# First expert stage of a two-block model: the first block's hidden products and the next gather placed ahead of the further blocks

## The chip, the cores and the metric

The kernel runs on one core of one Trainium2 chip. The metric is the time of one execution on the device in microseconds (us); lower is better. It computes in float32 throughout the part that is changed.

## The reference

Two model blocks in a row work on 256 tokens of width 1024: each is a token mixer (attention, in the first also a state-space branch) and then a mixture of experts. The change touches the first mixture alone. Each token chooses experts of one group among 32, and each expert is a gated unit of width 256:

```
def expert_block(args):
    xb, e = args
    return (jax.nn.silu(xb @ w_gate[e]) * (xb @ w_up[e])) @ w_down[e]

ys = lax.map(expert_block, (xs, blk_e)).reshape(P, D)
out = jnp.zeros((N, D), jnp.float32).at[buf_t].add(ys.astype(jnp.float32) * buf_w[:, None])
```

Here `xs` are the chosen tokens of each expert, and `buf_w` the weight with which a result is added back to its token.

## The kernel before, in words

**Groups and blocks.** The first expert stage handles the 32 experts in 8 groups of 4. The four experts of a group share TensorE's columns, 32 tokens each, so that one *block* serves 4 x 32 tokens. If an expert has more than 32 tokens, its group has *further blocks*. How many is counted on the chip (`block_tables`, L2119) and read from the small table `tabI` by each engine with two loads (L452, L453). `run_experts` (L446) is the loop that TensorE, ScalarE and VectorE all run: four passes with two groups each (u = 0 and 1); in each group first `begin`, then an `If` (L455) around the further blocks, and then the first block (`first`).

**Steps of a block on TensorE.** `gather_group` (32 products of the tokens `hN` with a matrix of ones and zeros) brings the block's tokens together; `hidden_group` (L1082, 128 products: 64 with the gate weights, then 64 with the up weights) fills one PSUM bank; `act_turn` and `spread_turn` transpose the activations and the matrix that spreads results; `down_group` (L1093, 32 products) and `scatter_group` (16 products) add the result to the tokens' sums. The first block is pipelined over groups: its tokens are gathered one group earlier (`gather_group` in `first`, L1189), and its results are scattered in the next group's `first` (L1194). A further block runs all its steps at once, ahead of the first block of its group, and waits between them for VectorE and ScalarE.

**Steps on the other engines.** VectorE makes the matrices of ones and zeros (`gather_onehot`, L2159; `spread_onehot`, L2170 and L2171), copies the hidden products out (`units`, L2204), half of the gathered tokens (`pair_out`, L2188) and the results (`ys_out`, L2194). ScalarE takes the sigmoid (L1681), the other half of the gathered tokens (L1669) and the transposed matrices. Each engine takes its instructions in order.

**Weights.** A ring of 12 slots of 1 MB holds exactly one group: 4 gate, 4 up and 4 down tiles. SyncE asks for the next group's tiles in that order (`load_moe1`, L484). It waits for a slot to come free in `free1` (L494): gate tiles for `gates_used`, which the first block's 64th hidden product counts up (L1090), up tiles for `hidden`, down tiles for `down`, all of the first block, which runs last in its group:

```
def free1(j, groups):
    sp.wait_ge((gates_used, s1["hidden"], s1["down"])[j // 4], groups)
```

After the eight groups SyncE asks for the tiles of the next dense stage with the same `free1`, for the slots that the last group leaves. The second expert stage (32 experts, `GROUP[2]` = 1) uses `run_experts` too.

## Time and profile before

| | us |
|---|---|
| median of 3 runs | 2052.98 |
| lowest and highest of them | 2050.46, 2053.23 |
| the profiled execution's own time | 2053.45 |
| its span (first to last instruction) | 2051.7 |
| TensorE busy in the span | 1832.5 (89%) |
| VectorE, ScalarE busy | 527.4, 390.7 |
| moved by the DMA engines | 626.77 MB, mean 305 GB/s |
| first expert stage, first gather to last scatter | about 433 to 726 |

Times in the views are microseconds from the span's start. PE is TensorE's array, PEld its weight loads (PEldq its sequencer), DVE VectorE, ACT ScalarE, SPq SyncE's queue. All matrix products carry L464, a helper's line, and all transposes L592, so that the steps are told apart by their tiles and counts: hidden products are x128 with 256 columns out of `ring`, down products x32 with 512, gathers x32 out of `hN`, scatters x16. The "idle before" of an instruction ends with what released it; "issue" means that the profile shows nothing it waited for. PEclk is the granted clock of TensorE as a share of 2.4 GHz.

### The profile page before, as it was taken

To read this page: it belongs to the slowest core of one execution; us is meant where nothing else is said; L and a number is where in the kernel's file an instruction comes from. 1 tells how busy PE (TensorE), PEld (TensorE's weight loads), DVE (VectorE), ACT (ScalarE), POOL (GpSimd) and SP (SyncE) were. 2 spreads that over 40 slices of the span, in tenths; PEclk is the share of its full clock that TensorE was granted. 3 is DMA by queue.
4 is the path that set the end of the run, shared out by engine and by line. 5 is a ranking of instruction groups with operands and counts; after the bars stand their busy time and mean duration, and the time that the engine had idled before them with its cause. 6 is when DMAs were issued, how large, how long until landed. Compare 5 with 4: busy or idle time off the path is not lost.

```text
span 2051.7 us, 27907 instructions
## 1 busy us (share of the span) xinstructions
PE 1832.5 (89%) x10699; PEld 1006.3 (49%) x10700; DVE 527.4 (26%) x1211; ACT 390.7 (19%) x905; POOL 50.2 (2%) x109
## 2 busy tenths in 40 slices
PE   6999899978667889999978999889988999989887
PEld 4665677855344566777844333333333333323332
DVE  3676332131111133232431111111111111111112
ACT  3132454021011130244020111111100111101111
POOL 0040000000000010010010000000000000000000
PEclk9999899998888999999989999999999999999999
DMA  9968622418999662232435999999999899999997
GB/s 399 403 230 346 271 82 84 162 63 334 394 411 409 267 215 87 65 100 98 152 149 208 416 417 417 417 417 418 416 416 419 323 418 417 416 417 417 416 416 297
DMA packets 108632, 626.77 MB, mean 305 GB/s; under 512 B 11200, under 2 KB 15296, under 8 KB 50080
## 3 DMA queue, kind: packets, MB, share of 16 engines
q1 hardware_dynamic: 106688, 620.10, 75.1%
q0 software_dynamic: 1584, 4.33, 1.3%
q8 instruction: 70, 1.15, 0.2%
q10 hardware_dynamic: 272, 1.05, 0.1%
q14 instruction: 18, 0.15, 0.0%
HBM read 624.39 MB, written 1.05 MB: 305 GB/s over the span
## 4 chain that ended last, share of the span: by engine, by line
PE 62%; DMA 20%; SPq 10%; issue 4%; DVE 2%; ACT 1%; DVEq 0%; ACTq 0%
PE ps L464 59%; DMA ring<-in_w_gu_dram 15%; SPq L517 5%; SPq L520 4%; PE ps L592 2%; DMA ring<-in_moe_w_gate_dram 1%; DMA ring<-in_w_dn_dram 1%; DMA ring<-in_ada_w_dram 1%; DMA ring<-in_w_mod_dram 1%; DMA ring<-in_moe_w_down_dram 1%; ACT arena L1403 1%; PE ps L839 0%; SPq L490 0%; SPq L421 0%; ACT hT L1730 0%
## 5 line engine op out<-in xcount | busy, mean ns | idle before, releaser
L464 PE MATMUL ps<-ring,arena 128*64 128x512 f32 (+2 forms) x5376 | 898.8, 558 | 123.7 <-issue 59.1
L464 PEld LDWEIGHTS ps<-ring,arena 128*64 128x64 f32 (+1 forms) x5376 | 291.7, 131 | 671.4 <-issue 482.2
L464 PE MATMUL ps<-arena 64*128 64x512 f32 (+11 forms) x1494 | 262.2, 417 | 36.7 <-ACT arena L1403 15.5
L464 PE MATMUL ps<-hT,ring 128*128 128x256 f32 (+1 forms) x960 | 237.2, 402 | 2.3 <-DVE hT L1864 2.3
L464 PEld LDWEIGHTS ps<-hT,ring 128*128 128x128 f32 x960 | 180.5, 192 | 58.8 <-issue 33.6
L464 PEld LDWEIGHTS ps<-arena 64*128 64x128 f32 (+7 forms) x1494 | 128.2, 159 | 154.5 <-issue 97.0
L2212 DVE TENSOR_SCALAR arena<-ps 128x512 f32<-128x512 f32 (+1 forms) x34 | 23.0, 676 | 535.3 <-PE ps L464 535.3
L1403 ACT ACTIVATE arena<-ps 128x256 f32<-128x256 f32 (+5 forms) x191 | 104.3, 570 | 267.7 <-PE ps L592 134.0
L1669 ACT ACTIVATE arena<-ps,mod,gain 128x128 f32<-128x128 f32 x176 | 66.1, 458 | 425.3 <-PE ps L464 425.3
L1681 ACT ACTIVATE arena<-arena 128x512 f32<-128x512 f32 (+1 forms) x44 | 25.3, 575 | 601.7 <-DVE arena L2212 400.7
L464 PEld LDWEIGHTS ps<-arena,hN 128*128 128x128 f32 x960 | 116.3, 200 | 42.2 <-issue 16.3
L464 PE MATMUL ps<-arena,hN 128*128 128x128 f32 (+1 forms) x960 | 124.8, 287 | 10.3 <-DVE arena L2159 5.7
L464 PE MATMUL ps<-ring,hT 128*128 128x256 f32 (+2 forms) x416 | 83.5, 380 | 5.8 <-ACT hT L1743 5.8
L592 PE MATMUL ps<-consts,arena 128*128 128x128 f32 x522 | 73.7, 278 | 9.2 <-DVE arena L2218 6.2
L464 PEld LDWEIGHTS ps<-ring,hT 128*128 128x128 f32 (+1 forms) x416 | 70.6, 187 | 19.3 <-issue 8.3
L2199 DVE COPY arena<-ps 128x512 f32<-128x512 f32 x34 | 23.5, 692 | 214.1 <-PE ps L464 214.1
L464 PE MATMUL ps<-arena,ring 128*128 128x256 f32 x352 | 76.5, 380 | 0.7 <-ACT arena L1403 0.7
L592 PEld LDWEIGHTS ps<-consts,arena 128*128 128x128 f32 x522 | 60.1, 142 | 31.9 <-issue 15.0
L464 PEld LDWEIGHTS ps<-arena,ring 128*128 128x128 f32 x352 | 66.7, 190 | 10.3 <-ACT arena L1403 0.9
L1576 ACT ACTIVATE arena<-ps,stat 128x15 f32<-128x15 f32 (+3 forms) x128 | 56.0, 447 | 79.3 <-DVE stat L1960 79.3
L1960 DVE TENSOR_REDUCE stat<-ps 128x2 f32<-128x1024 f32 (+3 forms) x40 | 36.7, 917 | 129.4 <-PE ps L464 129.4
L464 PE MATMUL ps<-hN,ring 128*128 128x256 f32 x256 | 56.4, 380 | 0.0
(286 smaller groups left out, 876.1 us busy)
## 6 DMA issues: line engine op xcount, KB each, us to landing
ring<-in_w_gu_dram SPq DMA_DIRECT2D x256, 1024.0 KB, 20.3
ring<-in_w_dn_dram SPq DMA_DIRECT2D x128, 1024.0 KB, 23.1
ring<-dense_dram SPq DMA_DIRECT2D x56, 1024.0 KB, 12.2
ring<-in_moe_w_gate_dram SPq DMA_DIRECT2D x32, 1024.0 KB, 8.2
ring<-in_moe_w_up_dram SPq DMA_DIRECT2D x32, 1024.0 KB, 16.0
ring<-in_moe_w_down_dram SPq DMA_DIRECT2D x32, 1024.0 KB, 14.6
ring<-in_ada_w_dram SPq DMA_DIRECT2D x24, 1024.0 KB, 18.5
ring<-in_w_mod_dram SPq DMA_DIRECT2D x24, 1024.0 KB, 8.5
```

What stands on the lines that cost most here:

```text
L464: ins = nc.tensor.matmul(*a, start=start, stop=stop, **k)
L517: sp.dma_start(ring[:, i % RING, :], src).then_inc(full[i % RING], 16)
L520: sp.dma_start(slot_ap(i, (2, D)), src).then_inc(full[i % RING], 16)
L592: return nc.tensor.transpose(dst, src, ident[0:src.shape[0], 0:src.shape[0]])
L1403: return a(dst, src, ACT.Copy, scale=scale)
L1576: last = a(e_[:, s * nk:s * nk + m], ps[:, bank, at:at + m], ACT.Exp, bias=stat[:, i % 2, s:s + 1], accum_out=stat[:, i % 2, 4 + s:5 + s])
L1669: last = a(dst[:, d, :], ps[:, bank, k * P:(k + 1) * P], ACT.Identity, scale=gs[:, d:d + 1], bias=sh[:, d:d + 1])
L1681: a(sg[:, 0:w], glu[:, 0:w], ACT.Sigmoid, scale=1.702 if n == 2 else 1.0).then_inc(s["sig"], 1)
L1960: V.tensor_reduce(dst, sc[:, :, :, 0:m], AX.X, ALU.max, negate=True).then_inc(madeV, mark(madeV, ("mx", n, i)))
L2199: V.tensor_copy(dst, ps[:, 3, :]).then_inc(s["ys"], 1)
L2212: ts(glu[:, 0:w], ps[:, 1, 0:w], 7.0, None, ALU.min).then_inc(s["glu"], 1)
```

## The change

In `run_experts`, `begin` of the first stage is called ahead of the two table loads and the `If`. On TensorE, VectorE and ScalarE it now holds the first block's hidden products, its units, the next group's gather and the turn of the spreading matrix; the further blocks follow, and then the first block's activation turn, scatter and down products. Since a further block now runs between the first block's units and its `act_turn`, it writes its activations to a buffer of its own (`act_more`).

The gate and up slots are free when the hidden products of the first block and of all further blocks up to this group are done. SyncE waits for both counts ahead of the first gate tile (j = 0) and for nothing ahead of the up tiles; `gates_used` is gone. The count of further blocks comes from a new row of `tabI`, which `block_tables` fills with a running sum plus one. The one stands for a count that VectorE gives once at the start, and for which its `units` waits are raised by one. Ahead of the down tiles (j = 8) it waits for `down` of the first block. The second expert stage keeps its order. The diff, cut to its core:

```diff
@@ -320,6 +320,7 @@
         act = M(512)
+        act_more = M(256)
@@ -441,7 +442,6 @@
         used2 = sem("moe2_rows_used")
-        gates_used = sem("moe1_gate_weights_used")
@@ -449,9 +449,12 @@
                     g = it * 2 + u
+                    if n == 1:
+                        begin(it, u, g)
...
                     before = eng.value_load(tabI[0:1, 1, bass.ds(g, 1)], min_val=0, max_val=E * (MAXB[n] - 1))
-                    begin(it, u, g)
+                    if n == 2:
+                        begin(it, u, g)
@@ -491,18 +494,30 @@
-            def free1(j, groups):
-                sp.wait_ge((gates_used, s1["hidden"], s1["down"])[j // 4], groups)
+            def free1(j, groups, blocks):
+                if j == 0:
+                    sp.wait_ge(s1["hidden"], groups)
+                    sp.wait_ge(S[1, "more"]["hidden"], blocks)
+                elif j == 8:
+                    sp.wait_ge(s1["down"], groups)
+            def blocks_until(group):
+                return sp.value_load(tabI[0:1, 0, bass.ds(group + 8, 1)], min_val=1, max_val=E * (MAXB[1] - 1))
             load_moe1(0, lambda j: sp.wait_ge(freed, moe1_at + j - RING + 1))
+            sp.wait_ge(madeV, nth(madeV, ("tables", 1)))
             with sp.Fori(1, E // 4) as group:
-                load_moe1(group, lambda j: free1(j, group))
+                blocks = blocks_until(group - 1)
+                load_moe1(group, lambda j: free1(j, group, blocks))
+            blocks = blocks_until(E // 4 - 1)
...
                     groups, j = divmod(at - RING - moe1_at, 3 * GROUP[1])
-                    free1(j, groups + 1)
+                    free1(j, groups + 1, blocks)
@@ -1068,7 +1083,7 @@
-            def act_turn(n, s):
+            def act_turn(n, s, act):
@@ -1079,15 +1094,13 @@
-            def hidden_group(it, u, s, xs, first):
+            def hidden_group(it, u, s, xs):
...
                                       w[x][:, k, :], start=k == 0, stop=k == KD - 1)
-                    if n == 0 and first:
-                        last.then_inc(gates_used, 1)
@@ -1164,17 +1177,30 @@
+                def begin(it, u, p):
+                    pe.wait_ge(s["xs"], p * 2 + 2)
+                    hidden_group(it, u, s, xsP)
+                    pe.wait_ge(s["gather_onehot"], p + 2)
+                    pe.wait_ge(s["ys"], p + 1)
+                    gather_group(s, ohgF)
+                    pe.wait_ge(s["spread"], p + 1)
+                    pe.wait_ge(s["spread_onehot"], p + 1)
+                    spread_turn(s, ohsF, 3, T)
...
-                    pe.wait_ge(s["ys"], p + 1)
+                    pe.wait_ge(s["xs"], p * 2 + 4)
...
                     gather_group(x, ohgM)
+                    pe.wait_ge(s["act"], p + 1)
                     pe.wait_ge(x["xs"], q * 2 + 2)
-                    hidden_group(it, u, x, xsM1, False)
+                    hidden_group(it, u, x, xsM1)
+                    pe.wait_ge(s["spread"], p + 2)
...
                     pe.wait_ge(x["act"], q + 1)
-                    act_turn(2, x)
+                    act_turn(2, x, act_more)
@@ -1183,23 +1209,13 @@
-                    hidden_group(it, u, s, xsP, True)
-                    pe.wait_ge(s["gather_onehot"], p + 2)
-                    pe.wait_ge(s["ys"], p + 1)
-                    gather_group(s, ohgF)
-                    pe.wait_ge(s["spread_onehot"], p + 1)
-                    spread_turn(s, ohsF, 3, T)
+                    pe.wait_ge(s["spread"], p + 2)
                     pe.wait_ge(s["act"], p + 1)
-                    act_turn(2, s)
+                    act_turn(2, s, act)
...
                     pe.wait_ge(s["actT"], p + 1)
-                    pe.wait_ge(s["spread"], p + 2)
...
-                def begin(it, u, p):
-                    pe.wait_ge(s["xs"], p * 2 + 2)
-                    pe.wait_ge(s["spread"], p + 1)
@@ -1673,22 +1689,42 @@
                         half_out(s, 0, xsP, 0)
-                    if n == 1 and s is x:
+                    if n == 1:
...
                     a(sg[:, 0:w], glu[:, 0:w], ACT.Sigmoid, scale=1.702 if n == 2 else 1.0).then_inc(s["sig"], 1)
-                    if n == 1 and s is not x:
-                        act_.wait_ge(s["gathered"], q + 1)
-                        half_out(s, 1, xsP, 2)
-                    act_.wait_ge(s["turned"], q)
-                    copy(actT.rearrange("p a b -> p (a b)")[:, 0:w], ps[:, 3, 0:w]).then_inc(s["actT"], 1)
+                    turned_out(s, q, w)
...
                         half_out(s, 1, xsP, 0)
+                    spread_out(s, q, onehotT)
+                def turned_out(s, q, w):
+                    act_.wait_ge(s["turned"], q)
+                    copy(actT.rearrange("p a b -> p (a b)")[:, 0:w], ps[:, 3, 0:w]).then_inc(s["actT"], 1)
+                def spread_out(s, q, onehotT):
...
+                def begin(it, u, e):
+                    act_.wait_ge(s["glu"], e + 1)
+                    a(sg[:, 0:256], glu[:, 0:256], ACT.Sigmoid).then_inc(s["sig"], 1)
+                    act_.wait_ge(s["gathered"], e + 2)
+                    half_out(s, 1, xsP, 2)
+                    spread_out(s, e + 1, ohtF[u % 2])
+                def first(it, u, e):
+                    if n == 1:
+                        turned_out(s, e + 1, 256)
+                    else:
+                        block_of(s, e + 1, ohtF[u % 2], it if u == 1 else None)
@@ -1697,8 +1733,11 @@
                 act_.wait_ge(madeV, nth(madeV, ("tables", n)))
-                run_experts(act_, n, lambda it, u, e, q, b: block_of(x, q + 1, ohtM),
-                            lambda it, u, e: block_of(s, e + 1, ohtF[u % 2], it if n == 2 and u == 1 else None))
+                further = lambda it, u, e, q, b: block_of(x, q + 1, ohtM)
+                if n == 1:
+                    run_experts(act_, 1, further, first, begin)
+                else:
+                    run_experts(act_, 2, further, first)
@@ -2126,6 +2165,8 @@
                 step(V.tensor_tensor_scan(c1, cst("ones", 0, N)[0:1], c0, 0.0, ALU.mult, ALU.add))
+                if n == 1:
+                    ts(tabI[0:1, 0, 8:8 + N], c1, 1.0, None, ALU.add)
@@ -2203,7 +2244,7 @@
                     w = 512 if n == 2 and s is not x else 256
-                    v.wait_ge(s["hidden"], q)
+                    v.wait_ge(s["hidden"], q + 1 if n == 1 and s is x else q)
@@ -2215,7 +2256,8 @@
                     v.wait_ge(s["sig"], q)
-                    tt_(act[:, 0:w], lin[:, 0:w], sg[:, 0:w], ALU.mult).then_inc(s["act"], 1)
+                    dst = act_more if n == 1 and s is x else act
+                    tt_(dst[:, 0:w], lin[:, 0:w], sg[:, 0:w], ALU.mult).then_inc(s["act"], 1)
@@ -2229,26 +2271,31 @@
-                def first(it, u, e):
+                def begin(it, u, e):
                     units(s, e + 1)
-                    if n == 1:
-                        v.wait_ge(s["gathered"], e + 2)
-                        pair_out(s, xsP)
-                        gather_onehot(s, ohgF, e + 2, slots0)
-                    else:
-                        select(esel16[(u + 1) % 2], e + 1)
+                    v.wait_ge(s["gathered"], e + 2)
+                    pair_out(s, xsP)
+                    gather_onehot(s, ohgF, e + 2, slots0)
...
+                def first(it, u, e):
+                    if n == 2:
+                        units(s, e + 1)
+                        select(esel16[(u + 1) % 2], e + 1)
+                        v.wait_ge(s["spreadT"], e + 1)
+                        spread_onehot(s, ohsF, e + 1, slots0)
...
                 V.memset(crow[:, 3, 0:1], 0.0).then_inc(s["spread"], 1)
+                if n == 1:
+                    V.memset(crow[:, 3, 1:2], 0.0).then_inc(x["hidden"], 1)
@@ -2260,7 +2307,10 @@
                 gather_onehot(s, ohgF, n, slots0, n)
-                run_experts(v, n, further, first)
+                if n == 1:
+                    run_experts(v, 1, further, first, begin)
+                else:
+                    run_experts(v, 2, further, first)
```

## Rows read from the trace of the kernel before

**Rows 1.** stretches: engines' busy us, then PEclk, DMA share, GB/s

```profile
470.00:500.00 30.00, 21.83 (x210) 13.41 (x206) 5.03 (x12) 2.47 (x7) 0.00 (x0) 0.79 0.99 401
527.65:531.70 4.05, 4.05 (x40) 2.22 (x44) 0.00 (x0) 0.00 (x0) 0.00 (x0) 0.50 1.02 419
```

**Rows 2.** SyncE's timeline: start, us, gate tiles of groups 1, 2, 3 and 5

```profile
469.70 2.50 SPq L490 DMA_DIRECT2D ring<-in_moe_w_gate_dram  x4
...
500.56 2.09 SPq L490 DMA_DIRECT2D ring<-in_moe_w_gate_dram  x4
...
533.53 3.36 SPq L490 DMA_DIRECT2D ring<-in_moe_w_gate_dram  x4
...
595.01 2.43 SPq L490 DMA_DIRECT2D ring<-in_moe_w_gate_dram  x4
```

**Rows 3.** TensorE's timeline, groups 0 to 2: start, us, operation, [idle before]

```profile
432.95 5.38 PE L464 MATMUL ps<-arena,hN 128*128 128x128 f32 x32 [0.28 <-DVE arena L2159]
441.48 3.84 PE L464 MATMUL ps<-arena,hN 128*128 128x128 f32 x32 [3.15 <-DVE arena L2159]
447.21 7.12 PE L464 MATMUL ps<-ring,arena 128*32 128x256 f32 x128 [1.89 <-ACT arena L1669]
...
457.11 3.64 PE L464 MATMUL ps<-ring,arena 128*32 128x512 f32 x32 [0.79 <-ACT arena L1403]
...
489.57 2.78 PE L464 MATMUL ps<-ring,arena 128*32 128x256 f32 x22 [5.42 <-issue]
495.10 9.13 PE L464 MATMUL ps<-ring,arena 128*32 128x256 f32 x106 [2.75 <-issue]
...
511.82 3.64 PE L464 MATMUL ps<-ring,arena 128*32 128x512 f32 x32
527.65 9.13 PE L464 MATMUL ps<-ring,arena 128*32 128x256 f32 x128 [12.19 <-issue]
```

**Rows 4.** sequencer branches, ns: first stage's If, its loop, second's If

```profile
L455 PEldq COMPARE_BRANCH  x8: 84/5784/6027, 440.0 to 670.3; - x8
...
L449 PEldq COMPARE_BRANCH  x4: 73/6118/6672, 512.8 to 717.8; - x4
...
L455 PEldq COMPARE_BRANCH  x32: 68/208/436, 1051.7 to 2007.1; - x32
```

**Rows 5.** DMA queues from 470 to 691 us: packets, MB, share of 16 engines

```profile
q8 instruction: 29, 0.48, 0.9%
```

**Rows 6.** VectorE's timeline, group 0 and ahead of group 7's block

```profile
472.98 0.42 DVE L2208 COPY arena<-ps 128x256 f32<-128x256 f32 x1 [10.89 <-PE ps L464]
...
478.93 0.43 DVE L2171 TENSOR_TENSOR arena<-arena 128x256 f32<-128x256 f32 x1 [0.17 <-issue]
...
671.20 0.69 DVE L2196 COPY arena<-ps 128x512 f32<-128x512 f32 x1 [4.86 <-PE ps L464]
...
672.93 0.43 DVE L2159 TENSOR_TENSOR arena<-consts,arena 128x256 f32 x1 [0.44 <-issue]
```

**Rows 7.** issues, us to landing (min/median/max), groups 2 and 4

```profile
L490 SPq DMA_DIRECT2D ring<-in_moe_w_down_dram x1: 379/379/379, 516.9 to 516.9; - x1
...
DMA to landing us min/median/max: 5.3/11.3/17.2
...
L490 SPq DMA_DIRECT2D ring<-in_moe_w_down_dram x2: 379/722/1066, 578.3 to 578.8; - x2
...
DMA to landing us min/median/max: 6.3/17.0/19.0
```

**Rows 8.** the chain of waits: the stream's last tile

```profile
672.57 18.50 DMA ring<-in_moe_w_down_dram
```

**Rows 9.** TensorE's timeline at the stage's end, groups 7 and after

```profile
673.41 3.84 PE L464 MATMUL ps<-arena,hN 128*128 128x128 f32 x32 [2.28 <-DVE arena L2159]
...
691.21 5.80 PE L464 MATMUL ps<-ring,arena 128*32 128x512 f32 x32 [2.96 <-DMA ring<-in_moe_w_down_dram]
...
721.83 3.72 PE L464 MATMUL ps<-arena 128*128 128x256 f32 x16 [1.41 <-DVE arena L2197]
```

More of the change, by code:

```diff
@@ L1223, in further @@
                     pe.wait_ge(x["act"], q + 1)
-                    act_turn(2, x)
+                    act_turn(2, x, act)
                     pe.wait_ge(x["spread_onehot"], q + 1)
@@ L1244, in first @@
                     pe.wait_ge(s["act"], e + 1)
-                    act_turn(4, s)
+                    act_turn(4, s, act)
                     spread_turn(s, ohsF, 1, 0)
```

## Prediction, written before the changed kernel was run

> **What bounds the kernel now.** I read the expert stage from the outside in. First its length and its load: from 470 us until the last of its weights is there, the DMA engines are busy all the time and move 401 GB/s over 30 us, 419 in a stretch without a gap [rows 1], while TensorE is busy 21.83 of those 30 us. A tile of 1.05 MB at 419 takes 2.5 us, so a group of twelve takes 30 us. Then SyncE's own timeline [rows 2]: the gate tiles of the groups are asked for at 469.70, 500.56, 533.53, 595.01 us, some 31 us apart: nearly, not quite, the 30 us of the stream. Then TensorE [rows 3]. Groups 0 and 7 hold one further block each (the gather of 32 ahead of the products, at 441.48 for group 0), groups 1 to 6 none. Its work in a plain group is 18.5 us; the rest is idle put down to "issue": 5.42 and 2.75 us in group 1, 12.19 us in group 2. The branches of its sequencer say what that is [rows 4]: the jump over the further block takes 5.8 us (median), the jump back to the loop's head 6.1 us, where the same `If` of the second expert stage takes 0.2 us. In the same stretch the queue for instructions moves 29 packets in the full DMA engines [rows 5]. So a taken jump waits for its code. The array stands 5.4 us after a jump over the block (the sequencer reaches it ahead of the array), 4.0 us after the jump back (511.82 + 3.64 = 515.46 to the 519.5 at which a branch of 6.7 us from 512.8 ends, the longest of rows 4), and 2.75 us more where the page after the target is late.
>
> The stage's end is set in three pieces, which I add up: when the stream starts, how often it runs dry, and what TensorE still has to do after its last tiles.
>
> Of such jumps the Trainium skill, "Runtime: NRT & Kernel Launch", section on instruction fetch mechanics, says that TensorE's instruction memory holds 2048 instructions and that a jump out of the prefetched pages stalls on a fetch. By its second half the trace is right; by the first, the loop body of some 1,800 instructions (424 products and transposes in each half, two instructions each, and the waits) would stay resident, the jumps would cost nothing from the second pass on, and moving them would change nothing. The branch rows of this stage decide against that half: they are long in every pass with plain groups.
>
> **Part 1, start of the stream.** Before, group 0 runs its further block whole, then the first block's gate products, and asks for group 1's gates at 469.70. After, it runs the first block's hidden products, the next gather, the turn, then the further gather and hidden products, and asks then. The first gather ends at 438.33 [rows 3]; its copy to the weights' side takes the 1.89 us that stands ahead of 447.21: 440.2. Hidden 7.1: 447.3. From there to the further gather the chain goes through VectorE [rows 6]: units, copies and one-hots of the first block reach their last instruction 5.95 us after the hidden products (472.98 to 478.93), then two table loads and a branch: the further one-hot starts 1.73 us after the copy ahead of them (671.20 to 672.93) and takes 0.43. With 0.1 of signalling that is 8.2 us; TensorE's own gather and turn take 4.2 of them, so it stands 4.0 us where before it stood 3.15. Then gather 3.84, 1.89, hidden 7.11, issue 0.3: 468.7, which is 1.0 us earlier. A stall like it puts TensorE at 1.2 GHz: the gather at 432.95, behind the router's short waits, takes 5.38 us, the others 3.84. I take +1.5 for that. Part 1: +0.5 us, bounds -1.0 and +2.
>
> **Part 2, the stream's gaps.** With a full queue tiles land 2.5 us apart. From group 2 to 3 the last down tile lands at 516.9 + 17.2 = 534.1 and the next gate tile, asked for at 533.53, at 533.5 + 5.3 = 538.8, 2.2 us later than it could. From group 4 to 5: 578.8 + 19.0 = 597.8 and 595.0 + 6.3 = 601.3: 1.0 us [rows 7]. Both are groups with the jump back and the jump over ahead of their hidden products (12.19 us idle). Groups with one jump there lose nothing. After, the jump over the block comes behind the gather; ahead of the hidden products of even groups stand 4.0 us, of odd ones none. The gates are asked for 3.6 us later relative to their products (all 128 instead of 64), but tiles of downs still queued (10 us of stream) cover that, if hidden products end no later than 7.3 us after the up tiles land. For group 2: let U be the landing of group 1's ups. Hidden(1) ends at U + 3.6; gather and turn 4.2, jump 5.4, activation turn, scatter and down 7.5, low clock in those 1.7, jump back 4.0, hidden(2) 9.13 as at 527.65 (its first 4 us at 1.2 GHz, a granted clock of 0.50 [rows 1]): U + 35.5. The limit is U + 30 + 7.3. So no gap: -3.2 us. If the cover is gone, by +2.75 of a late page or low clock throughout (+1.8 more), each even group gives a gap instead; bounds -3.2 and +5. I take -3.2, since counting the body's instructions puts the page ends far behind both jump targets.
>
> **Part 3, the tail of group 7.** The last down tile lands at 672.57 + 18.50 = 691.07 [rows 8], so the last up tile at 681.1. Before, the further block's hidden products run then, its down products wait for the last tile (2.96 us, and low clock: 5.80 for 3.64), and the last scatter ends at 721.83 + 3.72 = 725.55 [rows 9]: 44.4 us after the ups. After, the first block's up products come first. From the ups: 3.6; VectorE's chain to the further gather 8.2; gather 3.84; 1.89; hidden 7.11; turn, activation and copy to the down products 2.8 (454.33 to 457.11); down 3.64; 1.40; scatter 3.72; activation turn and scatter 3.8; down 3.64; 1.40; scatter 3.72. That sums to 48.8, and 50.3 with a gather at 1.2 GHz in the stall. The wait for the down tiles is gone, but a stall of 4.0 us stands between the gather and the further block. Before, VectorE's one-hot cost TensorE 2.28 us (ahead of 673.41), and under the stream. Part 3: +5.9 us, bounds +2 and +7.
>
> **Costed at nothing:** SyncE's loads of a count (it waits for the hidden products anyway); one more VectorE operation of 0.2 us in the tables (covered by TensorE's first gather to 438.33); the memset; `act_more`. Moved past SyncE's queue: up tiles no longer have a wait of their own, so they are asked for with the gates, behind 10 us of queued tiles. Down tiles are asked for 18.8 us after the hidden products, where it was 11.2 (504.23 to 515.46); for group 2's that is 7.6 us before its ups have landed, with tiles still queued. The next stage's loads come some us sooner and are not waited for. The second expert stage keeps its order; its branches of 0.2 us show that its code is at hand.
>
> **Sum:** +0.5 - 3.2 + 5.9 = +3.2 us on the profiled execution (2053.45, span 2051.7), which stands 0.5 above the median shown: 2056 us.
>
> **Rivals.** (a) *Clearly slower:* TensorE's chain outgrows the stream. The jump's stall now lies between gather and down; the margin of 1.8 us in part 2 goes if a page end falls near either target (2.75) or the clock stays at 1.2 GHz through scatter and down (1.8 more than taken). Worst, 2.7 us of gap in each of three even groups: +0.5 + 8.1 + 5.9 = +14.5, 2067. For it: 5.42 and 2.75 stand side by side in group 1 today. Against: the code's layout changes. It decides above 33.7 us from hidden(1) to hidden(2). (b) *Faster:* the order frees the stream and VectorE's stall stays warm. From the first landing (5 us after 469.70, as at 533.53) to the last at 691.07 are 216.4 us, 9 above 83 x 2.5; 3.2 of it are the gaps, the rest goes with landings stretched beside code fetches. Were that 5.8 gone too, and no clock lost: 3.2 - 5.8 - 3.0 = -5.6, 2047.5. Against: as much code is fetched as before. (c) *Nothing lands:* the gains and the tail cancel exactly (part 1 at -1.0, a tail of +4.2): 2053.
>
> **How the numbers follow.** A change under 0.2% (4.1 us) can't be told from none. Forecast with (c) 0.5, all within 0.2%. The forecast's own upper part with (a) 0.36, slower. (b) 0.14, faster. The range takes (b)'s end and (a) up to two thirds of its price: 2047.5 to 2064.
>
> **What would show it.** Right: TensorE's idle "issue" ahead of hidden products about 4 us in even groups and none in odd ones, 5 us behind the gather in both; gates landing 2.5 us behind the downs; a wait of some 4 us on VectorE's L2159 ahead of both further gathers; last up tile near 678.5, end of the last scatter near 728.7. Wrong: gaps in the stream after even groups, or a further gather that starts at once.

## The result, and the profile after

The changed kernel takes 2057.79 us (median) against 2052.12 us for the kernel before on the same chip: ratio 1.003, 95% interval 1.0019 to 1.0042, so 4 to 9 us slower. The forecast was 2056.0 in a range of 2047.5 to 2064, with most of its chance on "within 0.2%" (0.5) and the rest mainly on slower (0.36). By the forecast's own mark of 0.2% that is "slower", if not by much: 0.3%, with an interval that begins just under 0.2%. One of the changed kernel's seven runs took 6499.1 us, alone among all the runs here; the ratio leaves it out, and its cause is not known.

The profiled execution has a span of 2053.6 us (its own time is 2055.46). In it the stage, from the start of the first gather to the end of the last scatter, takes 431.29 to 727.96, 296.7 us, where it was 292.6 (432.95 to 725.55). That is +4.1. What lies around it differs by -1.7 ahead of it and -0.5 behind it; the change touches neither.

TensorE's timeline of the kernel after (start, us, operation, idle before), against [rows 3] and [rows 9]:

```profile
431.29 5.54 PE L467 MATMUL ps<-arena,hN 128*128 128x128 f32 x32 [0.28 <-DVE arena L2200]
...
438.72 7.11 PE L467 MATMUL ps<-ring,arena 128*32 128x256 f32 x128 [1.89 <-ACT arena L1685]
...
454.51 5.86 PE L467 MATMUL ps<-arena,hN 128*128 128x128 f32 x32 [4.69 <-DVE arena L2200]
461.97 7.11 PE L467 MATMUL ps<-ring,arena 128*32 128x256 f32 x128 [1.60 <-ACT arena L1685]
...
471.88 5.34 PE L467 MATMUL ps<-ring,arena 128*32 128x512 f32 x32 [0.80 <-ACT arena L1419]
...
485.94 10.81 PE L467 MATMUL ps<-ring,arena 128*32 128x512 f32 x160
...
506.80 0.66 PE L607 MATMUL ps<-consts,arena 128*128 128x128 f32 x2 [6.06 <-issue]
507.25 4.97 PE L467 MATMUL ps<-arena 128*128 128x256 f32 x16
512.15 3.64 PE L467 MATMUL ps<-ring,arena 128*32 128x512 f32 x32
...
519.72 4.48 PE L467 MATMUL ps<-ring,arena 128*32 128x256 f32 x48 [3.93 <-issue]
525.17 4.52 PE L467 MATMUL ps<-ring,arena 128*32 128x256 f32 x80 [0.97 <-issue]
...
689.85 5.47 PE L467 MATMUL ps<-arena,hN 128*128 128x128 f32 x32 [4.25 <-DVE arena L2200]
696.91 7.11 PE L467 MATMUL ps<-ring,arena 128*32 128x256 f32 x128 [1.59 <-ACT arena L1685]
...
724.24 3.72 PE L467 MATMUL ps<-arena 128*128 128x256 f32 x16 [1.41 <-DVE arena L2238]
```

Read them from the top. Group 0's hidden products now come first (438.72), and the gather of its further block waits 4.69 us for VectorE's L2200 (a matrix of ones and zeros, in short a one-hot; L2200 here is L2159 in the kernel before). At the end of that wait TensorE is at 1.2 GHz, and the gather takes 5.86 us instead of 3.84. This is the stretches view of its first 3 us (engines' busy us, then granted clock, DMA share, GB/s):

```profile
454.50:457.50 3.00, 2.99 (x14) 2.99 (x15) 0.72 (x2) 0.00 (x0) 0.00 (x0) 0.50 0.00 0
```

In group 1 the hidden products follow the down products of group 0 without a pause (x160 is both). Behind the gather stand 6.06 us of "issue", the jump over the block. Group 2 has the jump back ahead of its hidden products, 3.93 us, and in their middle a short idle of 0.97 that is also put down to issue (a wait for the next page of code, as the prediction takes it; the view does not name it). In group 7 the same wait for VectorE comes again, 4.25 us. What VectorE does in that time (start, us, operation, idle before), against [rows 6]:

```profile
681.68 0.42 DVE L2249 COPY arena<-ps 128x256 f32<-128x256 f32 x1 [8.39 <-PE ps L467]
...
685.43 1.36 DVE L2232 TENSOR_SCALAR arena<-ps,gain,mod 128x128 f32<-128x128 f32 x4 [2.31 <-PE ps L467]
686.71 0.41 DVE L2200 TENSOR_TENSOR arena<-consts,arena 128x256 f32<-128x256 f32 x1
687.04 0.42 DVE L2211 TENSOR_TENSOR arena<-consts,arena 128x256 f32<-128x256 f32 x1
687.63 0.42 DVE L2212 TENSOR_TENSOR arena<-arena 128x256 f32<-128x256 f32 x1 [0.17 <-issue]
689.37 0.42 DVE L2200 TENSOR_TENSOR arena<-consts,arena 128x256 f32 x1 [1.32 <-issue]
```

The gathered tokens are copied at 686.8; then come the next group's one-hots (686.71 to 688.05), the two table loads and the branch (1.32 us of idle), and only then the one-hot that TensorE waits for.

The weight stream, SyncE's timeline and the times to landing behind group 2 (last down tile, next gate tile), against [rows 2, 7]; last its branches and the queue for instructions against [rows 4, 5]:

```profile
469.35 2.08 SPq L493 DMA_DIRECT2D ring<-in_moe_w_gate_dram  x4
...
496.96 2.67 SPq L493 DMA_DIRECT2D ring<-in_moe_w_gate_dram  x4
```

```profile
L493 SPq DMA_DIRECT2D ring<-in_moe_w_down_dram x1: 382/382/382, 518.3 to 518.3; - x1
...
L493 SPq DMA_DIRECT2D ring<-in_moe_w_gate_dram x1: 341/341/341, 529.9 to 529.9; - x1
...
DMA to landing us min/median/max: 6.3/10.8/15.4
```

```profile
L458 PEldq COMPARE_BRANCH  x8: 83/6122/6467, 449.4 to 685.0; - x8
...
L449 PEldq COMPARE_BRANCH  x4: 73/5986/6069, 513.1 to 720.2; - x4
...
q8 instruction: 29, 0.48, 0.9%
```

518.3 + 15.4 = 533.7 and 529.9 + 6.3 = 536.2: 2.5 us, no gap, where 2.2 us were lost. Jumps cost about what they did (median 6.1 against 5.8 us over the block), and as many pages of code are fetched.

### The profile page after: what moved, and what is told of

Read it like the earlier page. It is cut to its first block, busy times and chain, and to the rows that moved or that the text cites. A ratio compares the mean times of both kernels' runs of the same rounds, so it can differ in the third digit from the quotient of the medians.

```text
span 2053.6 us, 27940 instructions
## 1 busy us (share of the span) xinstructions
PE 1833.6 (89%) x10697; PEld 1014.9 (49%) x10700; DVE 527.1 (26%) x1213; ACT 388.9 (19%) x903; POOL 50.2 (2%) x109
## 4 chain that ended last, share of the span: by engine, by line
PE 60%; DMA 21%; SPq 10%; issue 3%; DVE 2%; ACT 2%; DVEq 1%; ACTq 0%
PE ps L467 58%; DMA ring<-in_w_gu_dram 15%; SPq L532 6%; SPq L535 4%; DMA ring<-in_moe_w_up_dram 3%; PE ps L607 2%; DMA ring<-in_w_dn_dram 1%; DMA ring<-in_ada_w_dram 1%; DMA ring<-in_w_mod_dram 1%; ACT arena L1419 1%; SPq L493 0%; ACT arena L1685 0%; DVEq L1886 0%; PE ps L854 0%; SPq L422 0%
## 5 line engine op out<-in xcount | busy, mean ns | idle before, releaser
L467 PE MATMUL ps<-ring,arena 128*64 128x512 f32 (+2 forms) x5376 | 884.1, 547 | 85.7 <-DMA ring<-in_w_gu_dram 50.0
L467 PE MATMUL ps<-arena 64*128 64x512 f32 (+11 forms) x1492 | 270.8, 423 | 36.7 <-ACT arena L1419 15.5
L467 PEld LDWEIGHTS ps<-arena 64*128 64x128 f32 (+7 forms) x1494 | 135.4, 163 | 156.8 <-issue 96.0
L1697 ACT ACTIVATE arena<-arena 128x512 f32<-128x512 f32 (+1 forms) x36 | 21.9, 610 | 415.9 <-DVE arena L2253 400.5
L607 PEld LDWEIGHTS ps<-consts,arena 128*128 128x128 f32 x522 | 60.5, 143 | 67.9 <-issue 50.8
L2240 DVE COPY arena<-ps 128x512 f32<-128x512 f32 x34 | 23.5, 692 | 214.1 <-PE ps L467 214.1
```

What stands on the lines that cost most here:

```text
L467: ins = nc.tensor.matmul(*a, start=start, stop=stop, **k)
L607: return nc.tensor.transpose(dst, src, ident[0:src.shape[0], 0:src.shape[0]])
L1697: a(sg[:, 0:w], glu[:, 0:w], ACT.Sigmoid, scale=1.702 if n == 2 else 1.0).then_inc(s["sig"], 1)
L2240: V.tensor_copy(dst, ps[:, 3, :]).then_inc(s["ys"], 1)
```

## The three pieces, kernel by kernel

A stage is the sum of: first gather to the request for group 1's gates; 4.8 to 5.1 us to the first landing; first to last landing of the 84 tiles of groups 1 to 7; less some 10 us from the last up tile to the last tile; last up tile to the last scatter. All are differences of starts, landings and ends in one profiled execution of each kernel. Medians are of all timed runs; in brackets is the median of the kernel before in the same comparison. Pages are the packets of the queue for instructions (q8) while the stream runs (one more or less by where its ends are put). Each row's three pieces come from one execution, and executions of one kernel differ: after and after_again are the same kernel.

| kernel | median us | stage | gates 1 asked for | first to last landing | last up tile to end | pages fetched |
|---|---|---|---|---|---|---|
| before | 2052.1 | 292.6 | 36.8 | 216.6 | 44.4 | 29 |
| after | 2057.8 [2052.1] | 296.7 | 38.1 | 213.6 | 50.1 | 29 |
| after_again | 2055.7 [2049.5] | 298.7 | 38.0 | 213.5 | 52.4 | 29 |
| loads_first | 2055.7 [2049.5] | 295.6 | 37.0 | 213.1 | 50.5 | 29 |
| onehots_late | 2052.9 [2049.5] | 289.9 | 35.4 | 213.3 | 46.3 | 29 |
| both | 2049.6 [2049.5] | 288.9 | 32.7 | 215.5 | 45.8 | 29 |
| gates_late | 2054.1 [2049.8] | 296.3 | 41.9 | 214.7 | 44.8 | 30 |
| gates_early | 2057.8 [2049.8] | 299.1 | 38.2 | 213.6 | 52.4 | 29 |
| z_before | 2006.3 [2049.9] | 246.5 | 18.2 | 213.1 | 20.2 | 31 |
| z_after | 2009.7 [2049.9] | 252.4 | 14.6 | 214.7 | 28.3 | 31 |
| n_before | 1995.3 [2049.9] | 236.4 | 11.3 | 208.5 | 21.9 | 3 |
| n_after | 2001.5 [2049.9] | 242.6 | 14.9 | 209.3 | 23.5 | 3 |
| single_before | 2045.5 [2050.7] | 286.2 | 38.5 | 208.3 | 44.6 | 2 |
| single_both | 2042.9 [2050.7] | 284.6 | 32.8 | 207.9 | 49.1 | 1 |

## Experiments

**z_before and z_after: no further block at all.** The counts of further blocks are set to zero in both orders, so what is left is the plain groups alone; tokens beyond 32 per expert are left out. Such kernels are read against each other, not against before.

```diff
                 step(ts(c0, c0, -MAGIC, 0.0, ALU.add, ALU.max))
+                if n == 1:
+                    step(ts(c0, c0, 0.0, None, ALU.mult))
```

> The order of before, with the counts of further blocks of the first expert stage set to zero, so that tokens beyond 32 per expert are left out there. To be read against z_after, not against before (the tokens of the second expert stage change). Theory (three pieces): gaps of 2.2, 1.0 and 0.4 us stay in the weight stream behind groups 2, 4 and 6, as in before; the stream starts at the gate half of group 0's hidden products, some 11 us behind the first gather; the stage ends about 24 us after the last up tile lands. Rival (the further blocks made the gaps): no gaps here.

> The order of after, with the same counts set to zero. Theory: against z_before the stream starts 3.6 us later (gates asked for after all 128 products), has no gaps (-3.4 us), and the stage ends 26 to 28 us after the last up tile, since the jump over the block now stands behind the gather (+2 to +4): in sum +1 to +5 us against z_before. Rival 1 (only the further blocks' wait for VectorE costs anything): 3 us faster than z_before. Rival 2 (TensorE's chain has outgrown the stream): gaps of 2 us or more behind even groups, 8 us slower.

Measured: 2006.28 and 2009.66 us, z_after 3.4 slower. The sum is in the range of +1 to +5, but its terms are not the expected ones. z_before has no gap in the stream (landings 2.5 us apart behind every group), against the theory, and asks for group 1's gates 18.2 us behind the first gather, not 11, because its jump over group 0's block stands ahead of the hidden products. z_after asks 3.6 us earlier, not later. The rest is the tail: 28.3 us against 20.2, since the jump of group 7 now stands behind the last up tiles. There it costs 8 us: 5.65 of idle, and a scatter at low clock behind it that takes 5.72 us where 3.62 would do. So the rival by which z_after would be 3 us faster, because only VectorE's wait costs anything, is out. In the kernel after, this price is not paid: its group 7 has a further block, and no idle put down to issue stands in its tail. That the gaps vanish in z_before says they are no property of plain groups; gates_late, below, tells more.

The first jump of z_before is made while the DMA engines are idle. The first row is of the stretches view (busy of each engine, granted clock, DMA share, GB/s), the others are TensorE's timeline and its sequencer's branch:

```profile
437.50:443.30 5.80, 0.00 (x0) 0.00 (x0) 1.64 (x5) 2.73 (x5) 0.00 (x0) 0.93 0.03 6
```

```profile
443.37 10.02 PE L464 MATMUL ps<-ring,arena 128*32 128x256 f32 x128 [5.97 <-issue]
```

```profile
L455 PEldq COMPARE_BRANCH  x1: 3916/3916/3916, 439.1 to 439.1; - x1
```

The branch takes 3.9 us with the DMA engines 3% busy. So full queues are not needed for a long jump, as the prediction's "in the full DMA engines" might suggest. What they add to one isn't shown: most branches in a full stream take about 6 us, but three of z_before's take 3.3 to 3.5, with the DMA engines as busy as ever. Here is one of them, with its stretch, and all eight:

```profile
L455 PEldq COMPARE_BRANCH  x1: 3320/3320/3320, 463.6 to 463.6; - x1
463.60:466.90 3.30, 1.03 (x12) 0.12 (x4) 1.29 (x2) 0.00 (x0) 0.00 (x0) 1.00 0.99 405
L455 PEldq COMPARE_BRANCH  x8: 3320/4678/6206, 439.1 to 642.5; - x8
```

**n_before and n_after: the same without the jump.** The `If` and the further blocks' code are left out of the first stage's loop; both compute what z_before computes.

```diff
-                    with eng.If(more > 0):
-                        with eng.Fori(0, more) as b:
-                            further(it, u, g, before + b, b + 1)
+                    if n == 2:
+                        with eng.If(more > 0):
+                            with eng.Fori(0, more) as b:
+                                further(it, u, g, before + b, b + 1)
```

> z_before with the branch and the code of the further blocks left out of the first stage's loop on all engines; it computes what z_before computes. Theory (a taken jump waits for its code page): no idle of 5 us or more ahead of the hidden products, the gaps of the stream gone, so at least 3 us faster than z_before. If the code pages also stretch the landings of tiles (about 5.8 us over the stage), the first-to-last landing shrinks to about 208 us and it is 9 to 10 us faster. Rival (the idle is a wait for weights): nothing changes.

> z_after without the branch and the further blocks' code. Theory: the jump's 5.4 us behind the gather goes, which counts once, in the tail: 5 to 7 us faster than z_after, and 5.8 more if pages stretch the landings. Against n_before it is then 3.6 us slower (gates asked for later at the start) or equal. Rival (jumps cost nothing where the stream bounds, tail too): same as z_after.

Measured: 1995.30 and 2001.54 us, 11.0 and 8.1 below z_before and z_after. In both the first-to-last landing falls by about 5 us, to 208.5 and 209.3, and 83 steps of 2.5 us from tile to tile are 207.5: the code pages do stretch landings. In z_before and z_after one landing per pass of the loop takes 3.9 or 4.0 us (z_after has one more), and likewise in after_again, onehots_late and gates_early (3.6 to 4.0); after and loads_first have one such and then pairs of 3.0 to 3.4 us instead. In the two n_ kernels there is one such in all. The rest of n_before's gain is the start (18.2 to 11.3, against a tail 1.7 us longer), of n_after's the tail (28.3 to 23.5). TensorE's waits have other names now. The queue of instructions and a group of n_before:

```profile
q8 instruction: 3, 0.05, 0.1%
```

```profile
486.45 3.66 PE L465 MATMUL ps<-ring,arena 128*32 128x256 f32 x64 [2.31 <-DMA ring<-in_moe_w_gate_dram]
496.42 5.12 PE L465 MATMUL ps<-ring,arena 128*32 128x256 f32 x64 [6.31 <-DMA ring<-in_moe_w_up_dram]
```

"issue" has gone; TensorE waits for weights, as it should where the stream bounds. That shows that the idle put down to issue comes with the branch and the fetched code, and the rival (a wait for weights) is out. n_after is 6.2 us slower than n_before, not the 3.6 or less expected: 3.6 of the stage's 6.2 are the later request at the start, 0.8 lie in the stream and 1.7 in the tail, and the expectation had priced the last two at nothing.

**after_again, loads_first, onehots_late, both: what is VectorE's wait worth?** loads_first puts the two table loads ahead of `begin` on all engines; onehots_late moves the next group's one-hots behind the further blocks on VectorE; both does both.

```diff
@@ loads_first
-                    if n == 1:
-                        begin(it, u, g)
                     more = eng.value_load(...)
                     before = eng.value_load(...)
-                    if n == 2:
-                        begin(it, u, g)
+                    begin(it, u, g)
                     with eng.If(more > 0):
@@ onehots_late, VectorE
                 def begin(it, u, e):
...
                     pair_out(s, xsP)
-                    gather_onehot(s, ohgF, e + 2, slots0)
-                    v.wait_ge(s["spreadT"], e + 1)
-                    spread_onehot(s, ohsF, e + 1, slots0)
                 def first(it, u, e):
+                    if n == 1:
+                        gather_onehot(s, ohgF, e + 2, slots0)
+                        v.wait_ge(s["spreadT"], e + 1)
+                        spread_onehot(s, ohsF, e + 1, slots0)
```

> The changed kernel once more, as the one the next three are read against. 2055 to 2060 us, 4 to 6 above before.

> After, with the two table loads of a group put ahead of the first block's part on all engines, as in before; the If stays behind it. Theory (the further gather waits for VectorE's one-hot, and 1.7 us of that are the two loads and the branch): TensorE's stall ahead of both further gathers falls from 4.3 and 4.7 to about 3 us; 1.5 us each, so 2 to 3 us faster than after. Rival (the stall has another cause, the jump or the gather's copies): stalls unchanged, same time.

> After, with VectorE's two one-hots for the next group moved from ahead of the further blocks to behind them. Theory: they take 1.8 us (478.01 to 479.36 and a drain) out of the same chain: stalls of about 2.8 instead of 4.3 and 4.7 us, 2 to 4 us faster than after. Rival (TensorE waits for the next group's one-hots at its next gather instead): a new wait ahead of the gather behind the hidden products, and no gain.

> Both edits. Theory: the stall ahead of the further gathers is down to the copies of the gathered tokens, 1.4 to 1.9 us, and too short for low clock: the tail is 4 us shorter and the stream starts 3 to 4 us earlier, so 6 to 8 us faster than after and 1 to 3 us faster than before. Rival (the stalls are not what after lost): it stays above before.

TensorE's timeline at group 7's further gather, in loads_first, onehots_late and both:

```profile
680.92 3.84 PE L464 MATMUL ps<-arena,hN 128*128 128x128 f32 x32 [2.85 <-DVE arena L2197]
```

```profile
685.55 3.84 PE L467 MATMUL ps<-arena,hN 128*128 128x128 f32 x32 [2.04 <-DVE arena L2200]
```

```profile
687.02 3.84 PE L464 MATMUL ps<-arena,hN 128*128 128x128 f32 x32 [1.57 <-DVE arena L2197]
```

The stall falls from 4.25 us to 2.85, 2.04 and 1.57: each edit takes part of it away, onehots_late more than expected (2.8), and in all three this gather runs at 3.84 us again instead of 5.47. In group 0, which sets the start of the stream, the stall of 4.69 us falls to 2.96, 2.49 and 1.57, but there the gather is back at 3.84 in both alone; in loads_first it takes 6.64 us, in onehots_late 5.44. The times: onehots_late 2052.93 (ratio to before 1.0012, interval 1.0003 to 1.0022) is 2.8 us below after_again (2055.72), within the 2 to 4 expected. both, 2049.57 (1.000, 0.9991 to 1.0009), is 6.2 below it, within the 6 to 8, but equal to before, not 1 to 3 faster. So where VectorE's one-hots and the table loads stand accounts, within these intervals, for all that the change lost. loads_first has the same median as after_again (2055.69) though its stage is 1.1 to 3.1 us shorter in the profile; its ratio of 1.0042 (1.0029 to 1.0056) does not tell it from after_again's 1.0036, so alone it is not shown to gain anything. In both, the stream starts 5.3 us earlier than in after, and 2 us of that are lost in it (215.5 against 213.6; one landing of 3.7 us behind a group's last tile among them).

**gates_late and gates_early: when the gate slots are released.** gates_late takes the change's later release alone into the kernel before; gates_early takes the earlier release into the kernel after.

```diff
@@ gates_late
-                sp.wait_ge((gates_used, s1["hidden"], s1["down"])[j // 4], groups)
+                sp.wait_ge((s1["hidden"], s1["hidden"], s1["down"])[j // 4], groups)
@@ gates_early, in free1 (gates_used counted up as in the kernel before)
                 if j == 0:
-                    sp.wait_ge(s1["hidden"], groups)
+                    sp.wait_ge(gates_used, groups)
                     sp.wait_ge(S[1, "more"]["hidden"], blocks)
+                elif j == 4:
+                    sp.wait_ge(s1["hidden"], groups)
```

> Before, with the gate tiles asked for when all 128 hidden products of the first block are done, not the first 64: the change's later release alone. Theory (in before the gates of even groups are asked for with no queue left): each is 3.6 us or more later; gaps of 4 to 6 us behind even groups, 1 to 3 us behind odd ones, and the start 3.4 us later: 18 us slower than before, at least 12. Rival (the queued down tiles cover it, as in after): no more than 4 us slower.

> After, with the gate tiles asked for after the first block's first 64 hidden products (and the further blocks of the groups so far), the up tiles after all: the release of before in the order of after. Theory (in after the queue never runs dry): the stream has no gap to save, so the same time as after, within 1.5 us. Rival (the later release is part of the loss): 3 us faster or more.

gates_early: 2057.83 us (1.0035, 1.0022 to 1.0047), the same as after, as expected. gates_late: 2054.13 us (1.0017, 1.0007 to 1.0027), 4.3 us above before, not 18. SyncE's timeline of gates_late:

```profile
473.47 2.12 SPq L490 DMA_DIRECT2D ring<-in_moe_w_gate_dram  x4
503.95 2.54 SPq L490 DMA_DIRECT2D ring<-in_moe_w_gate_dram  x4
536.43 2.69 SPq L490 DMA_DIRECT2D ring<-in_moe_w_gate_dram  x4
```

Its stream starts 5.1 us later behind the first gather (41.9 against 36.8) and then has no gaps: first to last landing 214.7 instead of 216.6. So the theory that each gap belongs to its group and grows with the delay is wrong. What the rival allowed came about (4.3 us where it said at most 4), and its cover by queued tiles was there, but only because the stream itself was later: group 3's gates were asked for 2.4 us before the last queued tile landed, at 538.8. TensorE's pass over two groups is about as long as the stream's. In before, the hidden products of groups 4 and 6 start

```profile
589.17 9.09 PE L464 MATMUL ps<-ring,arena 128*32 128x256 f32 x128 [11.81 <-issue]
...
651.01 8.89 PE L464 MATMUL ps<-ring,arena 128*32 128x256 f32 x128 [11.57 <-issue]
```

and those of group 2 at 527.65 [rows 3]: passes of 61.5 and 61.8 us, with no wait for a tile in them. The stream's pass without gaps, stretched landings included, is 61.4 us (from z_before's first gate landings of groups 3 and 5, 517.9 and 579.3). In before the stream started so early that TensorE was behind it in group 2, a gap opened, and from then on the two were nearly in step (2.2, 1.0, 0.4 us). Start it later, and the gap isn't needed. Here a gap gave back 1.9 us of the 5.1 that the earlier start had won.

**single_before and single_both: code that stays.** Both orders with one group per pass in TensorE's loop, a body of some 900 instructions instead of 1,800. So that one body serves all groups, the transposed spreading matrix of each group has a place of its own (nine instead of two); `oht(at)` is one of the nine.

```diff
+                with eng.Fori(0, E // GROUP[n]) as g:
+                    more = eng.value_load(...)
+                    before = eng.value_load(...)
+                    begin(g, 0, g)
+                    with eng.If(more > 0):
+                        with eng.Fori(0, more) as b:
+                            further(g, 0, g, before + b, b + 1)
+                    first(g, 0, g)
...
-                pe.wait_ge(full[i % RING], it * 32 + 16 * (i // RING + 1))
+                pe.wait_ge(full[i % RING], it * 16 + 16 * (i // RING + 1))
...
-                    scatter_group(s, ysF1, ohtF[(u + 1) % 2])
+                    scatter_group(s, ysF1, oht(p))
```

> The order of before, with TensorE's loop of the first stage holding one group per pass instead of two (some 900 instructions instead of 1,800), and the transposed spreading matrices in nine places instead of two, so that one body can serve all groups. Theory (the jumps wait for code that is no longer held, and the fetched pages stretch the stream): about 2 fetches as in n_before, no idle of 4 us or more put down to issue, landings from first to last in 208 to 210 us instead of 216.6, a start 0 to 1 us earlier: stage 7 to 10 us shorter, 2040 to 2044 us. Rival (the body with both jumps still does not stay): as before, 2050 us.

> The kernel both (the change, loads first and one-hots late) with the same single body on TensorE. Theory: stream 208 to 210 us as in single_before; the start as in both (gates of group 1 asked for some 33 us behind the first gather instead of 37), no jump behind the gather, the tail 44 to 46 us: 3 to 5 us below single_before, 2036 to 2041 us. Rival (what the order gains at the start it gives back at the end once the jumps are free): equal to single_before within 1.5 us.

Measured: single_before 2045.49 us (0.9975, 0.9966 to 0.9985) and single_both 2042.86 us (0.9966, 0.9955 to 0.9977), with 2050.74 for before: 5.3 and 7.9 us faster, the only kernels here that do the whole work and beat before. single_both's sequencer branches, its queue of instructions, and TensorE's timeline in group 3, at group 7's further gather and at the last scatter:

```profile
L457 PEldq COMPARE_BRANCH  x8: 77/208/213, 447.8 to 674.2; - x8
```

```profile
q8 instruction: 1, 0.02, 0.0%
```

```profile
547.50 5.31 PE L478 MATMUL ps<-ring,arena 128*32 128x256 f32 x64 [6.31 <-DMA ring<-in_moe_w_up_dram]
...
677.96 3.84 PE L478 MATMUL ps<-arena,hN 128*128 128x128 f32 x32 [1.57 <-DVE arena L2211]
...
712.42 3.72 PE L478 MATMUL ps<-arena 128*128 128x256 f32 x16 [1.41 <-DVE arena L2249]
```

The same branches, 8 of them, take 0.2 us instead of 6.1. The landings take 208 us from first to last, as expected. single_before's median is 1.5 us above the range expected, single_both's 1.9 above its own; single_before's start came 1.7 us later, not earlier, and single_both's tail is 49.1 us, where 44 to 46 were expected. single_both lies 2.6 us below single_before, between theory (3 to 5) and rival (1.5). Their intervals against before overlap. Set against each other, the runs of the two differ by 2.4 us in the mean (95% interval 0.7 to 3.9): with the jumps free and VectorE's order mended the new order is probably the better one, by how much is open. The pieces say why it isn't much: the stream starts 5.7 us earlier (32.8 against 38.5), and the tail is 4.5 us longer (49.1 against 44.6). In the old order the further block's gather and most of its gate products run under the stream's last tiles; in the new one gather and hidden products of the further block, 11 us, all follow them. Some of those 4.5 us are clock: behind a wait of 6.33 us for the last up tile the up products take 5.18 us instead of 3.66, and the first down products take 5.34 instead of 3.64.

## Why the prediction was right

The sum was near and its terms were of the right sign and order; the chances did less well, with 0.5 on "within 0.2%" and 0.36 on what came, slower. Step by step, each against the stage of the profiled executions:

- *Part 1, start of the stream*, +0.5 forecast: 36.8 to 38.1, +1.3. The size is 0.8 off: VectorE's chain from the hidden products to the further gather takes 454.51 - 445.83 = 8.7 us, not 8.2, and the gather at low clock 5.86 instead of the 5.34 taken. The mechanism was as put.
- *Part 2, the gaps*, -3.2 forecast: 216.6 to 213.6, -2.9, with no gap behind groups 2, 4 and 6. The size was right, and the step's reason was half right. That the moved jump brings the hidden products of group 2 forward is so: from the request for group 1's gates to that for group 3's are 60.5 us (469.35 to 529.89) where it was 63.8 [rows 2], though all 128 products are now waited for. But the margin was thinner than put: from the end of hidden(1) to that of hidden(2) are 32.9 us (496.8 to 529.7), where 31.9 were forecast and 33.7 was the limit, which left 0.8 us of a margin of 1.8. And "each even group gives a gap" when the margin is gone is not how it goes: gates_late shows that whether a gap opens depends on how early the stream starts against TensorE. Parts 1 and 2 should have been one term. Whether the three gaps of 2.7 us that rival (a) priced would each have been lost, no run shows.
- *Part 3, the tail*, +5.9 forecast: 44.4 to 50.1, +5.7; after_again 52.4. The edits of both take 4.3 us of that back, 50.1 to 45.8. So of the 5.7 some 4 are the wait of TensorE for VectorE with the low clock behind it, and the rest is more work left behind the last up tiles. after_again has 2.3 us more in the tail than after, all of it clock: gather 6.00 us against 5.47, first down products 5.34 against 3.64. The prediction put 1.5 us of low clock there.
- *Costed at nothing*: the later release of the gates holds (gates_early, same time). The later requests for down tiles hold too: 489.65 for group 1, with up tiles still landing until 493.
- *Sum*: +3.2 forecast, +4.1 in the profiled stage, +5.7 in the medians (+4 to +9 by the interval); after_again's stage is +6.1. The profiled execution of after is its fastest run. So the loss is some 2 us larger than forecast; the term that fell shortest is part 1, and the low clock behind VectorE's wait varies by 2 us between executions, which the single value of 1.5 did not allow for.
- *Rivals*: (a) did not come about, though it was nearer than put; the stall behind the gather was longer than put (5.5 to 6.1 us instead of 5.4) and low clock went through the scatter (4.97 us at 507.25, 3.72 at 724.24), but the stream stayed without gaps. (b) did not come about in the change, but its premise, that fetched pages stretch the landings by 5.8 us over the stage, is right: 5 us by the n_ kernels. (c), that gain and tail cancel exactly, did not come about either: +5.7. "What would show it" named the idle of 4 us in even groups, none in odd ones, the wait on L2159 (now L2200), an end near 728.7: 3.93, none, 4.69 and 4.25, 727.96. The last up tile came at 656.6 + 21.2 = 677.8 where 678.5 was put.

The weighing of the rule on code also held. The Trainium skill, "Runtime: NRT & Kernel Launch", section on instruction fetch mechanics, gives TensorE 2048 instructions. A loop body of 1,800 would fit into that, and yet it fetched 29 pages in three and a half passes here, while one of 900 fetched one or two in seven groups; the measurement decides.

## What to carry to other kernels

A step that is moved ahead of a conditional block takes its helpers' work with it: look at which engine makes the block's first operand, and what now stands ahead of that in its queue. A stage bound by a stream has two places where such work counts first, its start and what is left when the last tile lands. In between, a wait of TensorE costs something only where it makes the stream run dry, and such a gap gives back part of what an early start won (1.9 of 5.1 us here). Where "issue" stands ahead of an instruction behind a branch, look at the branch's own duration: if it is microseconds, try a smaller loop body: here, halving it gained 5.3 us in the old order, where no order of the steps in the long body gained anything.

## What was not expected of the hardware

A jump to code that is not at hand took 3.9 us with idle DMA engines and 3.3 to 7.6 us, mostly about 6, in a full stream; why four of these (three in z_before, one in gates_late) took under 3.5 was not found out. Twenty-nine fetched pages of 16 KB, 0.9% of the DMA engines' time [rows 5], cost the weight stream about 5 us in 213; in most of the kernels that fetch them one landing per pass takes 3.6 to 4.1 us instead of 2.5. Where between 900 and 1,800 instructions the loop ceases to stay was not tried, nor why one landing per pass is hit so much harder than the others.
